# A hybrid decoder's last output stage: the gated memory rows' turn and product are moved, and the group weights with them

## The reference

```python
qd, gd, mq, mg = split(rms_norm(x) @ w_in)
o_g, lse_g     = band_attend(qd[g], k[g], v[g])          # three dilation groups
w              = softmax over the groups of lse_g         # group weights, per head
dil_out        = sum_g(o_g * w[g]) * silu(gd)             # the mixed rows
q              = rms_norm(mq) * 128 ** -0.5
mem_out        = mem_attend(q, mem_kv) * silu(mg)         # the gated memory rows
out            = x + concat(dil_out, mem_out) @ w_out
```

## Time and profile before

| | us |
|---|---|
| median of three runs | 2722.89 (2721.72 to 2724.37) |
| profiled execution | 2719.55 |
| its span, first to last instruction | 2717.4 |

### The profile page before, as it was taken

One profiled execution on the slowest core, in us unless ns is written; L12 is line 12 of the kernel. 1 busy time (PEld: TensorE's weight loads), 2 busy tenths in 40 slices (PEclk: granted clock), 3 DMA queues, 4 the chain that ended last, 5 costly groups with the idle time before them and its releaser, 6 DMA issues.

```text
span 2717.4 us, 41295 instructions
## 1 busy us (share of the span) xinstructions
PE 2702.2 (99%) x14834; PEld 2259.7 (83%) x14834; DVE 1789.1 (66%) x3925; ACT 1112.9 (41%) x3346; POOL 383.1 (14%) x610
## 2 busy tenths in 40 slices
PE   9999999999999999999999999999999999999999
PEld 7788888888887888878888888888888889998887
DVE  7686766768678644435575667877674767777764
ACT  7533131212326234225434353532332349876632
POOL 0101010100101000000112032333424223210000
PEclk9999999999999999999999999999999999999999
DMA  8486555655676734324266676787768789757642
GB/s 281 143 250 208 183 167 179 207 182 171 210 246 207 222 115 156 101 97 152 94 246 228 211 268 216 274 284 264 247 237 284 262 311 330 231 177 262 217 154 82
DMA packets 292628, 567.75 MB, mean 209 GB/s; under 512 B 32432, under 2 KB 91760, under 8 KB 292424
## 3 DMA queue, kind: packets, MB, share of 16 engines
q1 hardware_dynamic: 257032, 462.31, 52.0%
q0 software_dynamic: 35392, 102.80, 10.6%
HBM read 432.28 MB, written 132.72 MB: 208 GB/s over the span
## 4 chain that ended last, share of the span: by engine, by line
PE 93%; DVE 4%; DMA 1%; ACT 1%; issue 1%; SPq 0%; DVEq 0%; ACTq 0%
PE ps L130 27%; PE ps L132 26%; PE ps L131 26%; PE ps L4133 2%; PE ps L3736 2%; PE ps L1385 1%; PE ps L4142 1%; PE ps L3774 1%; PE ps L3719 1%; PE ps L3035 1%; PE ps L3040 1%; PE ps L228 1%; PE ps L3130 1%; DMA a_raws<-w_mem_dram 0%; DVE a_wp L124 0%
## 5 line engine op out<-in xcount | busy, mean ns | idle before, releaser
L130 PE MATMUL ps<-b_wp,b_sring 128*128 128x512 f32 x640 | 250.5, 391 | 0.0
L131 PE MATMUL ps<-b_wp,b_sring 128*128 128x512 f32 x640 | 249.2, 389 | 0.0
L132 PE MATMUL ps<-b_wp,b_sring 128*128 128x512 f32 x640 | 249.1, 389 | 0.0
L130 PE MATMUL ps<-a_sring,a_wp 128*128 128x512 f32 x512 | 200.0, 391 | 0.0
L131 PE MATMUL ps<-a_sring,a_wp 128*128 128x512 f32 x512 | 199.3, 389 | 0.0
L132 PE MATMUL ps<-a_sring,a_wp 128*128 128x512 f32 x512 | 199.2, 389 | 0.0
L130 PE MATMUL ps<-b_wp,b_xthi 128*128 128x512 f32 x480 | 188.3, 392 | 0.0
L131 PE MATMUL ps<-b_wp,b_xthi 128*128 128x512 f32 x480 | 187.0, 389 | 0.0
L132 PE MATMUL ps<-b_wp,b_xtlo 128*128 128x512 f32 x480 | 186.7, 389 | 0.0
L1200 DVE TENSOR_TENSOR shared_o<-ps,b_spare 128x512 f32<-128x512 f32 x160 | 109.7, 685 | 112.3 <-PE ps L132 97.1
L1032 ACT ACTIVATE ps<-shared_o 128x128 f32<-128x128 f32 x390 | 103.4, 265 | 163.2 <-DVE shared_o L1200 146.0
(11 more groups left out here) (494 smaller groups left out, 6877.3 us busy)
## 6 DMA issues: line engine op xcount, KB each, us to landing
b_sring<-sums_dram SPq DMA_DIRECT2D x160, 512.0 KB, 5.2
a_sring<-sums_a_dram SPq DMA_DIRECT2D x128, 512.0 KB, 5.1
b_raws<-w_b_dram SPq DMA_DIRECT2D x176, 256.0 KB, 4.5
a_raws<-w_a_dram SPq DMA_DIRECT2D x140, 256.0 KB, 4.1
kv_dram<-shared_o POOLq DMA_DIRECT2D x96, 256.0 KB, 4.0
tok_b_dram<-shared_o POOLq DMA_DIRECT2D x96, 256.0 KB, 4.3
front<-tok_b_dram SPq DMA_DIRECT2D x96, 256.0 KB, 3.9
front<-grp_dram SPq DMA_DIRECT2D x48, 260.0 KB, 4.2
```

The costliest lines, as they stand in the source:

```text
L130: pe.matmul(acc, a_hi, b_hi, start=first, stop=False)
L131: pe.matmul(acc, a_hi, b_lo, start=False, stop=False)
L132: return pe.matmul(acc, a_lo, b_hi, start=False, stop=last)
```

## The change

In layer 1, for steps 2 to 15 (step 1 stays as it is):

- TensorE: `turn_o(t - 1)` no longer follows the scores. It stands in one block with `turn_mix(t)` (now first) and `turn_probs(t)`, and writes to bank 2. `left` is split: `left_begin(t - 1)` (mixed rows) stays in step t, `left_end` (gated memory rows) of that tile comes in step t + 1, where `right_end` stood. `right_end(t - 2)` moves behind the scores. `turn_query` waits for the low part of the query before and no longer for that of the gated memory rows.
- ScalarE: `weighted_sum` moves from amid the exponentials to the front, ahead of `query_high`; `high_o` moves to the end of the step.
- VectorE: `weights` moves ahead of `query_low`. `combine` is split: group 1 stands behind `gate`, group 2 and the multiply stay behind `maxima`. `add_left` takes tile t - 2 and stands ahead of `maxima`, `add_right` stands behind `combine`, `low_o` behind `mix_low`.
- The end: after the last step TensorE does `left_end(14)` and `right_end(14)`, then tile 15 as before; VectorE adds both halves of tile 14 before `low_o(15)`.

Layer 0 runs the same instructions in the same order as before.

```diff
@@ -3259,6 +3259,7 @@
 
         sums = ps[:, 3, :].rearrange("p (h e) -> p h e", h=H)
         turned_heads = ps[:, 0, :].rearrange("p (h t) -> p h t", h=H)
+        turned_o = lambda t: ps[:, 2 if t else 0, :].rearrange("p (h t) -> p h t", h=H)
         p_turned = ps[:, 3:5, :].rearrange("p a (b t) -> p (a b) t", t=P)
 
         @block.sync
@@ -3366,7 +3367,7 @@
                     of = og[:, :].rearrange("p (h t) -> p h t", t=P)
                 else:
                     act.wait_ge(oturned, t + 1)
-                    of = turned_heads
+                    of = turned_o(t)
                 act.activation(cat(0, t % 2)[:, MIX:KO, :], of, ACT.Copy).then_inc(ohi_done, 1)
 
             def dec_begin(t):
@@ -3439,23 +3440,24 @@
                 dec_begin(t)
                 if not conv and t > 1:
                     group_weights(t)
+                    weighted_sum(t)
                 if conv or t > 1:
                     query_high(t)
                 if conv:
                     mix_high(t)
                 for v in pair_at(t)[1:]:
                     dec.weigh(act, v)
-                high_o(t - 1)
+                if conv or t == 1:
+                    high_o(t - 1)
                 act.wait_ge(biased, t + 1)
-                exponentials(t, (0, 1))
-                if not conv and t > 1:
-                    weighted_sum(t)
-                exponentials(t, (2, 3)).then_inc(exped, 1)
+                exponentials(t, range(H)).then_inc(exped, 1)
                 for v in pair_at(t + 1)[:1] if not conv else ():
                     dec.weigh(act, v)
                 probs_first(t)
                 if not conv:
                     mix_high(t)
+                    if t > 1:
+                        high_o(t - 1)
                 for v in pair_at(t + 1)[:1] if conv else ():
                     dec.weigh(act, v)
             first()
@@ -3517,10 +3519,10 @@
                                   cstat[:, 2, :].rearrange("p (g h) -> p g h", h=H),
                                   cstat[:, 4:5, 0:H].to_broadcast([P, 3, H]), ALU.mult).then_inc(ops, 1)
 
-            def combine(t):
+            def combine(t, groups):
                 u = t % 2
                 dve.wait_ge(od_begun, t + 1)
-                for g in (1, 2):
+                for g in groups:
                     for h in range(H):
                         cols = slice(h * HD, (h + 1) * HD)
                         w = cstat[:, 5, g * H + h:g * H + h + 1]
@@ -3528,7 +3530,8 @@
                                                      in1=od[:, cols], op0=ALU.mult, op1=ALU.add)
                     m.then_inc(ops, 1)
                     sync_ops(t, 6 + g)
-                dve.tensor_tensor(od[:, :], od[:, :], gd_b[:, u, :], ALU.mult).then_inc(ops, 1)
+                if 2 in groups:
+                    dve.tensor_tensor(od[:, :], od[:, :], gd_b[:, u, :], ALU.mult).then_inc(ops, 1)
 
             def gate(t):
                 u = t % 2
@@ -3546,7 +3549,7 @@
 
             def low_o(t):
                 dve.wait_ge(ohi_done, t + 1)
-                of = og[:, :].rearrange("p (h t) -> p h t", t=P) if conv else turned_heads
+                of = og[:, :].rearrange("p (h t) -> p h t", t=P) if conv else turned_o(t)
                 dve.tensor_tensor(cat(1, t % 2)[:, MIX:KO, :], of, cat(0, t % 2)[:, MIX:KO, :], ALU.subtract
                                   ).then_inc(olo_done, 1)
 
@@ -3650,37 +3653,44 @@
                     query_low(t)
                 if not conv and t > 1:
                     joint_max(t)
+                    weights(t)
                 if t > (UNITS_UNTIL if conv else 1):
                     query_low(t)
                 if not (conv and t <= UNITS_UNTIL):
                     gate(t - 1)
-                if t >= 2:
+                if not conv and t > 1:
+                    combine(t, (1,))
+                if not conv and t > 2:
+                    add_left(t - 2)
+                if conv and t >= 2:
                     add_right(t - 2)
                 if conv or t > 1:
                     dec_middle(t)
                 maxima(t)
                 if not conv and t == 1:
                     low_o(0)
-                if not conv and t > 1:
-                    weights(t)
-                if conv or t > 1:
+                if conv:
                     low_o(t - 1)
-                if conv:
                     mix_low(t)
                 else:
-                    combine(t)
+                    combine(t, (2,) if t > 1 else (1, 2))
+                    if t >= 2:
+                        add_right(t - 2)
                 if not conv and t == 1:
                     dec_middle(t)
                 invert(t)
                 if conv and t <= UNITS_UNTIL:
                     keys.reduce(dve, 2 * t - 1)
-                add_left(t - 1)
+                if conv or t == 1:
+                    add_left(t - 1)
                 probs_second(t)
                 if not conv and t == 1:
                     dve.wait_ge(front.o_left, 1)
                     dec.setup(dve)
                 if not conv:
                     mix_low(t)
+                    if t > 1:
+                        low_o(t - 1)
                 dec_end(t)
             first()
             for t in range(1, NT):
@@ -3688,8 +3698,13 @@
             if follow:
                 dve.wait_ge(fresh, 1)
             gate(NT - 1)
-            low_o(NT - 1)
-            add_right(NT - 2)
+            if conv:
+                low_o(NT - 1)
+                add_right(NT - 2)
+            else:
+                add_left(NT - 2)
+                add_right(NT - 2)
+                low_o(NT - 1)
             if follow:
                 follow.clear_samples(dve)
                 follow.scale(dve, 0)
@@ -3713,10 +3728,10 @@
 
         @block.tensor
         def _(pe):
-            def turn(rows):
+            def turn(rows, bank=0):
 
                 for h in range(H):
-                    t = pe.transpose(ps[:, 0, h * HD:(h + 1) * HD], rows[:, h * HD:(h + 1) * HD], ident[:, :])
+                    t = pe.transpose(ps[:, bank, h * HD:(h + 1) * HD], rows[:, h * HD:(h + 1) * HD], ident[:, :])
                 return t
 
             def project(u, half, chunks):
@@ -3744,15 +3759,21 @@
             def turn_o(t):
 
                 pe.wait_ge(og_done, t + 1)
-                turn(og).then_inc(oturned, 1)
+                turn(og, 2 if t else 0).then_inc(oturned, 1)
+
+            def left_begin(t):
+                pe.wait_ge(mlo_done, t + 1)
+                pe.wait_ge(left_added, t)
+                project(t % 2, 0, range(MIX))
+
+            def left_end(t):
+                pe.wait_ge(olo_done, t + 1)
+                project(t % 2, 0, range(MIX, KO)).then_inc(left_done, 1)
 
             def left(t):
                 if t:
-                    pe.wait_ge(mlo_done, t + 1)
-                    pe.wait_ge(left_added, t)
-                    project(t % 2, 0, range(MIX))
-                pe.wait_ge(olo_done, t + 1)
-                project(t % 2, 0, range(MIX, KO)).then_inc(left_done, 1)
+                    left_begin(t)
+                left_end(t)
 
             def right_begin(t):
                 pe.wait_ge(right_added, t)
@@ -3837,7 +3858,7 @@
                 if conv:
                     pe.wait_ge(qlo_done, t)
                 else:
-                    pe.wait_ge(*((olo_done, t - 1) if t > 1 else (qlo_done, 1)))
+                    pe.wait_ge(*((olo_done, 1) if t == 2 else (qlo_done, t)))
                     pe.wait_ge(mlo_done, t)
                 turn(q_b[:, t % 2, :]).then_inc(qturned, 1)
 
@@ -3848,9 +3869,23 @@
                 if not conv and t > 1:
                     turn_query(t)
                 if t > 1:
-                    right_end(t - 2)
+                    if conv or t == 2:
+                        right_end(t - 2)
+                    else:
+                        left_end(t - 2)
                 dec_soft(t)
                 scores(t)
+                if not conv and t > 1:
+                    if t > 2:
+                        right_end(t - 2)
+                    left_begin(t - 1)
+                    dec_middle(t)
+                    turn_mix(t)
+                    turn_probs(t)
+                    turn_o(t - 1)
+                    right_begin(t - 1)
+                    dec_end(t)
+                    return
                 if not conv:
                     turn_o(t - 1)
                 if t == 1:
@@ -3867,6 +3902,8 @@
             for t in range(1, NT):
                 step(t)
             values(NT - 1)
+            if not conv:
+                left_end(NT - 2)
             right_end(NT - 2)
             if follow:
                 pe.wait_ge(fresh, 1)
```

## The result

The changed kernel takes 2731.42 us (median of 7 runs, 2729.67 to 2734.11) against 2721.80 us (7 runs): a ratio of 1.0032, with a 95% interval of 1.0022 to 1.0043. It is 9.6 us slower; 2732 was forecast, with +9.1. The profiled execution took 2732.85 us, 13.3 more than that of before, and its span is 13.7 longer. The output stage of layer 1, from the first turn of the probabilities to the start of the last matmul, takes 286.9 us (2437.54 to 2724.44) against 275.3 (2435.49 to 2710.78): 11.6 of the 13.7. Another 2.05 us lie ahead of the stage, where nothing was changed: over the ten profiled executions of this document the stage starts between 2435.49 and 2441.11.

A forecast was written before the change was run, and what follows sets the result against it. TensorE, busy almost without gaps, was taken as the bound. Waits of 10.19 us less 1.14 gave +9.1 on the profiled 2719.55, 2728.7; with 3.34 up to the median, 2732 us, own range 2729 to 2735, wider range 2724 to 2738.

The forecast's parts named there:

- the 1.03 us of waits: TensorE's waits before the turn of the mixed rows, forecast at 0.19 us in six steps; their removal would save 1.14 us.
- the term of the seams: Turning elsewhere than amid TensorE's projections might save two seams; taken as 0, between -0.1 and +0.1 us a step.
- bubbles: Rival: by the weight loads' share, 2.7 us of TensorE bubbles a step won in 14 steps, 2685 us; 2%.
- The path: From the start of VectorE's joint maximum through weights, weighted sum, query's copy and low part to TensorE's scores: 3.97 us.
- the block's work of 9.53: TensorE's own work from the start of a step's block of turns to the next scores, 9.53 us.
- Step 2's scores: TensorE's scores in step 2 of layer 1, forecast to start without a wait: 0.
- Step 5: TensorE's wait at the scores of step 5, forecast at 1.40 us, the same as for step 6.
- Step 4: TensorE's wait at the scores of step 4, forecast as the longest, 2.45 us, with about 0.5 for decode passes.
- The clock: Rival: TensorE's clock falls to the lower level in a tenth of eight waiting steps, 13.7 us more, 2746 us; 2%.
- Covered: Rival: VectorE has the query's low part ready in time, only the 1.14 us go, 2721.8 us; 9%.
- paid once: Rival: after the first wait other engines stay ahead, only steps 2 to 4 cost, 3.9 less 1.14, 2725.7 us; 7%.
- late decode values: Rival: the later store holds SP's queue and the weighing waits, 2 us in each of seven pairs, 2746 us; 4%.

The follow-up runs named there:

- e8: e2's kernel with, in step 2 of layer 1, the last three of right_end(0)'s twelve matmuls moved behind the scores; 2720.72 us, ratio 0.9995 to before.
- e2: The changed kernel with ScalarE's weighted sum moved back behind the query's copy; 2721.43 us, ratio 1.0000 to before.
- e3: The changed kernel with layer 1's joins of the decode values cut to 4 of 512 columns; 2725.37 us, ratio 1.0014 to before.
- e5: The changed kernel with one extra VectorE copy pass of 128x512 ahead of the joint maximum in steps 2 to 15; 2736.76 us, ratio 1.0051 to before.
- e1: The kernel before with only the weights and weighted sum moved ahead of the query's low part and copy; 2725.81 us, ratio 1.0013 to before.
- e6: The changed kernel with SP loading layer 1's decode values ahead of the store and the load of x; one run of 2733.40 us.
- e7: The changed kernel with VectorE's first combining and add_left put back behind the maxima; 2731.50 us, ratio 1.0031 to before.
- e4: The changed kernel's TensorE order, but probabilities turned first and mixed rows last, group weights in their old place; 2726.50 us, ratio 1.0018 to before.

## Why the prediction was right

*The bound.* TensorE stands at its limit in this stage, and little more than the 1.03 us of waits could be won. e8's stage wins 1.1: it still waits 0.27, so 0.8 of it are waits, and about 0.3 is the new order itself, 0.02 a step (e2, whose waits sum to 1.05, wins 0.4 in the same way). That is the term of the seams, put at nothing within 0.1 a step. No bubbles were there to be won, as the even starts had said against the share of weight loads.

*The path.* Its length was forecast to within 0.04 us in step 5, the block's work of 9.53 to within 0.02 (10.56 less the wait of 1.01), and e2, e3 and e5 shorten or lengthen it and move the waits with it. But for step 2, the steps that wait, and 9 to 11 and 13 to 15 that do not, are those forecast. In 9 to 11 the scores start 4.45 behind the joint maximum against 4.01 in step 5: 0.44 to spare, as forecast.

*Mis-sized terms.* The waits sum to 10.89 us against 10.19, and those that went to 1.03 against 1.14. Step 2's scores were taken to start on time and wait 0.90: at the end of step 1 VectorE still makes the decode path's new values ahead of the joint maximum, passes that the sum left out (e1 shows the same 0.90). In the changed kernel they go from 2450.95 on:

```profile
2450.95 0.33 DVE L2823 MEMSET dec_cat<- 128x320 f32 x1
...
2452.30 0.71 DVE L2866 SCALAR_TENSOR_TENSOR dec_nv<-dec_vn,front_skip,dec_nv 32x128 f32<-32x128 f32 x2
2452.94 0.15 DVE L3495 TENSOR_REDUCE front_cstat<-front 128x4 f32<-128x12 f32 x1
```

Step 5 was put at 1.40 and waits 1.01, step 6 at 1.40 for 1.22: the weighing releases ScalarE 1.56 and 1.80 behind the block (2502.40 - 2500.84 and 2520.85 - 2519.05), not 2.01. Step 4 was put at 2.45 and waits 1.98 for two other reasons. The copy starts 2.82 behind the block (2482.66 - 2479.84) where 2.56 and 0.5 for the decode path were taken; and TensorE has 9.89 us of its own work from there to the scores, not 9.53, because it also makes two small transposes of the decode path (L2724). In the profiled execution step 5's is 1.01 rather than e6's 1.16, because TensorE ran at the lower clock in step 4 and gave ScalarE time. The errors nearly cancel, +0.90, -1.04 and +0.84 in the other steps, and that is luck. So is part of how close 2732 came to 2731.42: its base, the median of three runs, lies 1.1 above that of seven, and +9.1 lies 0.5 below the +9.6 measured.

*The clock.* I gave it 2% and took short waits for harmless, and the prediction names its fall as a sign of being wrong. In the profiled execution it did fall, once, at a price of 1.5 us where the rival had 13.7; of the other executions there is no trace. The waits less the 1.03 give 9.9, and with the 1.5 that is 11.4 of the stage's 11.6. e6 has nearly the same waits without the fall, and its stage is 10.2 us longer than before: the price is that of the waits.

*Rivals.* Covered fell with the waits of all eight steps, paid once with steps 5 to 8, late decode values with e6.

## What to carry to other kernels

When an instruction moves ahead of another on an in-order engine, add up all that it waits for, across the engines, from the last instruction that each of them must finish first: here four passes of about 0.17 us, the exponential ahead of them and a scaling of 1.17 decided, not the big ones. An engine that is idle for a third of the time can still be late, if its work stands in the wrong order. And look at the first step of a carried-over pipeline by itself: it has less work to hide behind than the others.

## What was not expected of the hardware

The granted clock fell in mid-stage after a wait of about 2 us. TensorE in step 4 of the changed kernel: the scores' matmuls start 0.21 apart instead of 0.12, the next ones 0.43 instead of 0.23, until 2495.4:

```profile
2489.50 0.39 PE L132 MATMUL ps<-b_xthi,out_catlo 128*128 128x512 f32 x1
2491.71 0.36 PE L130 MATMUL ps<-b_xtlo 128*128 128x256 f32 x1 [1.82 <-DVE b_xtlo L3607]
...
2493.77 0.41 PE L131 MATMUL ps<-b_xtlo 128*128 128x256 f32 x1
2493.98 0.41 PE L132 MATMUL ps<-b_xtlo 128*128 128x256 f32 x1
2494.19 0.63 PE L130 MATMUL ps<-b_xthi,out_cathi 128*128 128x512 f32 x1
2494.62 0.63 PE L131 MATMUL ps<-b_xtlo,out_cathi 128*128 128x512 f32 x1
...
2495.43 0.39 PE L130 MATMUL ps<-b_xthi,out_cathi 128*128 128x512 f32 x1
```

Two windows of the same kernel (busy us of PE, PEld, DVE, ACT, POOL, then the granted clock). It is 0.50, the lower of the two levels (1.2 GHz), and then 1.00 again (2.4 GHz):

```profile
2492.00:2495.40 3.40, 3.40 (x15) 3.19 (x14) 3.30 (x9) 2.35 (x9) 0.00 (x0) 0.50 0.39 107
2495.40:2499.00 3.60, 3.60 (x17) 2.98 (x16) 2.94 (x9) 3.10 (x13) 0.00 (x0) 1.00 0.93 331
```

It costs 1.5 us: ten distances between starts of matmuls of 256 columns are 0.094 longer each, one is 0.03 longer, and three of 512 columns are 0.56 longer together. Against e6 the stage says the same: 1.4 longer, with 0.15 less of waits.

The same happened in e7 after step 8's wait of 2.06. It also happened near 867 us, long before the stage, in the profiled executions of e5 and e8, after waits of 1.99 and 1.96 for a VectorE instruction that the change leaves alone. In e8:

```profile
866.94 0.58 PE L130 MATMUL ps<-a_sring,a_xtlo 128*128 128x512 f32 x1 [1.80 <-DVE a_sring L124]
```

```profile
867.30:870.50 3.20, 3.20 (x9) 2.51 (x8) 3.13 (x10) 2.48 (x9) 0.08 (x1) 0.50 0.68 170
```

It did not happen after the changed kernel's own 2.07 in step 8, nor after e6's 1.99 and 2.06, e4's 2.05 and e1's 1.99 (at 867 us), nor after e5's 2.31 and 2.39. So all four falls followed a wait of about 2 us, and seven waits as long or longer brought none: the length of the wait alone does not decide, and what else does was not settled.
